# Expert rows by indirect DMA, five column-group products per row block, whole-row weights and halved mixer products in a hybrid decoder trunk

## The chip, the core and the metric

The kernel runs on one core of a Trainium2 chip. The metric is the device time of one launch in microseconds (us), as the median of several runs. Everything is computed in float32, and one launch does both layers.

## What is computed

There are two layers over 256 tokens of width 1024. Each layer has an RMSNorm, an input projection, four groups of token mixers, an output projection and a residual add, then a second norm and a feed-forward part: dense in the first layer, and in the second layer the best two of eight experts for every token. A final RMSNorm follows.

```python
def reference(x, ...):                       # x: (1, 256, 1024)
    for l in range(2):
        h = rmsnorm(x, attn_norm[l]); proj = h @ w_in[l]
        ...                                  # A window attention, B gated linear attention,
        ...                                  # C stick breaking, D RWKV-7, on 256 columns each
        x = x + mixed @ w_out[l]
        h = rmsnorm(x, ffn_norm[l])
        x = x + (swiglu(h, w1, w3, w2) if l == 0 else moe_swiglu(h, router, ...))
    return rmsnorm(x, final_norm)

def moe_swiglu(h, router, w1, w3, w2):
    top_vals, top_idx = lax.top_k(h @ router, 2)
    gates = jax.nn.softmax(top_vals)
    combine = ...                            # (tokens, 8): the gate, or zero
    for e in range(8):                       # w1, w3: 1024 x 1408, w2: 1408 x 1024
        out += combine[:, e:e+1] * ((silu(h @ w1[e]) * (h @ w3[e])) @ w2[e])
    return out
```

## The kernel before

Each engine runs a program of its own, written out by hand; the engines meet through semaphores. `full[b]` counts how often PSUM bank b has been filled, `free[b]` how often it has been emptied, and `nth(i, b, k)` is the count that belongs to the k-th use of bank b in round i of the expert loop. TensorE works through its list in order of the code; `mm` is the helper that records a product, so most products carry its line, L518. A float32 product shows as two weight loads and two matmul records in the profile.

**The mixers** (`layer_mixers`, `recurrence`, once a layer) are a long chain of small products. Many of them have 128 x 128 weights and only 64 columns of data: in `CO` (12 products), `GO` (8), `AO` (12), `RH0` and `RH1` (4 and 8), `U0` and `U1` (4 each), `Y0` and `Y1` (8 and 12), which is 72 products a layer; `BON` has 4 more with 2 columns. The router product `RT` (second layer alone) has 16 with 8 columns.

**The expert loop** (`experts` on TensorE, lines 975 to 1080) has one round per expert and pass; there are as many passes as are needed for 96 slots (`CAP`) per expert. In a round TensorE does four things:

- up: for each of the 11 blocks of 128 columns of w1 and w3, 8 + 8 products against `slot_h`, the 96 gathered tokens, each split in two halves of 64 output rows that stand at rows 0 and 64 of the bank (so 352 products in all);
- two transposes of `weigh` (the one-hot matrix with the gates, 256 tokens x 96 slots), and the gather for the next expert, 32 products of `tok` with the one-hot `pick`;
- down: for each of the 11 row blocks of w2, two products with 96 slots as output rows and 512 columns, into banks 2 and 3;
- the way back (`SCATTER`): four products of `weigh_t` with `slot_y`, 512 columns each, whose results VectorE adds to `x_sb`, the residual stream.

ScalarE takes the silu of one block at a time and VectorE multiplies it by the other factor. SyncE's queue loads the weights in pieces of 256 columns of w1 or w3 (lines of 1 KB) and of two row blocks of w2 (lines of 4 KB), through nine slots (`expert_slot`), each of which is loaded again when its last product is done.

Of the kernel before, what the change touches and what calls it, by code (L numbers as in the profile page):

```python
# [14 lines left out]
HALF = 64  # L15
D = 1024
# [37 lines left out]
MAX_PASSES = -(-SEQ // CAP)  # L54

# [3 lines left out]
for _name, _n in (("ident", 128), ("rev_cum", 128), ("rev_all", 128), ("c_mask", 128), ("a_mask", 256),  # L59
                  ("upper", 256), ("lower", 128), ("blk16", 128), ("off32", 128), ("off64", 128),  # L60
                  ("off128", 128), ("gla_mask", 64), ("same_head", 128), ("head_sel", 2),
                  ("reset64", 256), ("reset128", 512), ("inv_freq", 32), ("all", 128),
                  ("iota", CAP)):
    CONST[_name] = (_at, _n)
    _at += _n
# [19 lines left out]
def shape_constants():  # L85
# [25 lines left out]
    put("iota", np.arange(CAP)[None, :])  # L111
    put("inv_freq", (np.float32(ROPE_THETA) ** (-np.arange(0, HD, 2, dtype=np.float32) / np.float32(HD)))[None, :])
# [27 lines left out]
def psum_plan():  # L140
# [9 lines left out]
    for l in range(DEPTH):  # L150
# [24 lines left out]
        else:  # L175
            for name, bank in (("RT", 6), ("POS", 7), ("G0", 6), ("G1", 7)):
                use(name, l, bank)
# [16 lines left out]
def build(nc, t_in, out):  # L194
    ctx = ExitStack()
    with ctx:
# [13 lines left out]
        ring = sb("ring", [P, SLOTS, SLOT])  # L210
        region_e = sb("region_e", [P, 8192])
        region_f = sb("region_f", [P, 4096])
        region_g = sb("region_g", [P, 3072])
        region_m = sb("region_m", [P, 5128])
        normed = sb("normed", [P, 2, 512])
        ar = sb("ar", [P, 2, 2, NT, 256])
        c_q = sb("c_q", [P, 2, 2, SEQ])
        b_q = sb("b_q", [P, 4, SEQ])
        b_att = sb("b_att", [P, NT, 4, P])
        a_k = sb("a_k", [P, 2, SEQ])  # L220
# [85 lines left out]
        final_row = region_f[:, 1024:2048]  # L306

        W = MAX_PASSES * N_EXPERTS + N_EXPERTS
        slot_act = region_e[:, 0:UPC * CAP].rearrange("p (c s) -> p c s", c=UPC)
        slot_silu = region_f[:, 0:2 * CAP].rearrange("p (b s) -> p b s", b=2)  # L310
        slot_h = region_m[:, 0:KC * CAP].rearrange("p (c s) -> p c s", c=KC)
        pick = region_m[:, 768:768 + NT * CAP].rearrange("p (t s) -> p t s", t=NT)
        weigh = region_m[:, 960:960 + NT * CAP].rearrange("p (t s) -> p t s", t=NT)
        weigh_t = region_m[0:CAP, 1152:1152 + SEQ].rearrange("p (t n) -> p t n", t=NT)
        slot_y = region_m[0:CAP, 1408:1408 + D]
        place = region_m[:, 2432:2432 + NT * W].rearrange("p (t i) -> p t i", t=NT)
        chosen = region_m[:, 2432 + NT * W:2432 + 2 * NT * W].rearrange("p (t i) -> p t i", t=NT)
        share = region_m[:, 2432 + 2 * NT * W:2432 + 3 * NT * W].rearrange("p (t i) -> p t i", t=NT)
        count = region_m[:, 3072:3072 + N_EXPERTS]
        most = region_m[:, 3080:3088]  # L320
# [12 lines left out]
        descend = sb("descend", [P, N_EXPERTS])  # L333

# [47 lines left out]

        MORE = 3
        SLOTS_E = SLOTS + MORE
        more_slots = region_e[:, 8192 - MORE * SLOT:8192].rearrange("p (s n) -> p s n", s=MORE)
        more_landed = [ctx.enter_context(nc.semaphore(f"more_slot{i}_landed")) for i in range(MORE)]

        def expert_slot(k, n):

            r = k % SLOTS_E  # L390
            return ring[:, slot(FIRST_MOE + r), 0:n] if r < SLOTS else more_slots[:, r - SLOTS, 0:n]

        def expert_landed(i, k):

            r = k % SLOTS_E
            before = (FIRST_MOE + r) // SLOTS if r < SLOTS else 0
            s = landed[slot(FIRST_MOE + r)] if r < SLOTS else more_landed[r - SLOTS]
            return s, i * (16 * (E_PIECES // SLOTS_E)) + 16 * (before + k // SLOTS_E + 1)

# [4 lines left out]
        E_PIECES = 3 * UP2  # L404
        assert E_PIECES % SLOTS_E == 0


        per = [(UPC + 1) // 2, UPC // 2, 3, 2, 1, 1, 1, 1]
# [12 lines left out]
        def _(sp):  # L421
# [42 lines left out]
            def expert_piece(e, k):  # L464
                if k < 2 * UP2:
                    i = k // 2
                    m = min(256, D_FFE - 256 * i)
                    w = t_in["moe_w1" if k % 2 == 0 else "moe_w3"]
                    src = w[0, e].rearrange("(c p) n -> p c n", p=P)[:, :, 256 * i:256 * i + m]
                    dst = expert_slot(k, KC * m).rearrange("p (c n) -> p c n", n=m)  # L470
                else:
                    i = k - 2 * UP2
                    m = min(2, UPC - 2 * i)
                    src = t_in["moe_w2"][0, e].rearrange("(c p) n -> p c n", p=P)[:, 2 * i:2 * i + m, :]
                    dst = expert_slot(k, m * D).rearrange("p (c n) -> p c n", n=D)
                sp.dma_start(dst, src).then_inc(expert_landed(e, k)[0], 16)

            def expert_released(i, k):
                if k < 2 * UP2:
                    j = min(2 * (k // 2) + 1, UPC - 1)  # L480
# [1458 lines left out]
```

## Time and profile before

| | |
|---|---|
| median of 3 runs | 1143.0 us (1141.84 to 1143.22) |
| profiled execution | 1143.13 us, of which 1141.3 us from its first to its last instruction |
| TensorE busy | 1102.5 us of 1141.3 |
| granted TensorE clock, mean | 0.982 |
| start of the expert loop's first product | 689.28 us |
| one round of the expert loop | 55.09 us |
| time after the loop's last product | 9.63 us |

The time outside the profiled span is 1143.13 - 1141.3 = 1.8 us. Times in the rows of the profile count from the start of the span.

### The profile page before, as it was taken

The numbers are of one execution on the slowest core, as the hardware profiler recorded it, in microseconds if no ns is written. First come the engines' busy times: TensorE is split into PE (matmuls) and PEld (weight loads), VectorE is DVE, ScalarE is ACT, GpSimd is POOL, SyncE is SP. The second block draws the span as 40 slices with busy tenths as digits, with TensorE's granted clock in tenths as the row PEclk, the third lists the DMA queues.
The fourth block names the chain that finished last, engine by engine and source line by source line (L and its number), as shares of the span: only waits on it lengthen the run. The fifth ranks groups of instructions, "written<-read, shape, count | busy, mean of one in ns | idle before, by whom it ended". The sixth has DMA issues, their size and how long they took to land.

```text
span 1141.3 us, 22432 instructions
## 1 busy us (share of the span) xinstructions
PE 1102.5 (97%) x9790; PEld 837.2 (73%) x9790; DVE 285.3 (25%) x645; ACT 192.9 (17%) x444; POOL 61.4 (5%) x67
## 2 busy tenths in 40 slices
PE   8999999899999999999999969999999999999996
PEld 6887887488888543887789549595949494949592
DVE  4432473500000001233376341020111112021112
ACT  2244231100000001214323011011010111101011
POOL 2000411000000000000312100000000000000000
PEclk8999999999999999999999989999999999999998
DMA  9633101335554445343210256989898989899870
GB/s 325 196 122 105 43 1 38 111 117 160 160 159 167 156 148 155 119 135 109 74 38 1 74 185 203 343 279 351 287 344 289 343 293 323 305 301 332 279 272 37
DMA packets 168650, 213.34 MB, mean 187 GB/s; under 512 B 5120, under 2 KB 151200, under 8 KB 168480
## 3 DMA queue, kind: packets, MB, share of 16 engines
q1 hardware_dynamic: 166032, 210.29, 56.0%
q10 hardware_dynamic: 2576, 2.45, 0.7%
q8 instruction: 32, 0.52, 0.2%
q14 instruction: 10, 0.08, 0.0%
HBM read 211.67 MB, written 1.05 MB: 186 GB/s over the span
## 4 chain that ended last, share of the span: by engine, by line
PE 95%; DVE 3%; issue 1%; ACT 1%; POOL 0%; DMA 0%; DVEq 0%; POOLq 0%; ACTq 0%
PE bank L518 93%; PE bank L523 1%; DVE tok L1434 1%; POOL small L1343 0%; DMA x_sb<-in_x 0%; DVE b_att L1616 0%; DVE b_q L1413 0%; PE bank L1045 0%; DVE x_sb L1410 0%; PE bank L829 0%; ACT tok L1121 0%; DVE small L1425 0%; ACT hT L1133 0%; DVE hT L1410 0%; PE bank L797 0%
## 5 line engine op out<-in xcount | busy, mean ns | idle before, releaser
L518 PE MATMUL bank<-hT,ring 128*128 128x256 f32 (+1 forms) x1184 | 260.3, 382 | 0.0
L518 PEld LDWEIGHTS bank<-hT,ring 128*128 128x128 f32 (+1 forms) x1184 | 223.4, 189 | 36.1 <-issue 2.7
L518 PEld LDWEIGHTS bank<-region_m,ring 128*64 128x64 f32 x4096 | 170.3, 137 | 8.6 <-issue 8.6
L518 PE MATMUL bank<-region_m,ring 128*64 128x96 f32 x4096 | 173.7, 246 | 2.9 <-DVE region_m L1860 1.6
L518 PE MATMUL bank<-ring,region_e 128*96 128x512 f32 (+1 forms) x368 | 160.0, 594 | 0.0
L518 PEld LDWEIGHTS bank<-ring,region_e 128*96 128x96 f32 (+1 forms) x368 | 64.1, 176 | 89.5 <-issue 88.5
L518 PE MATMUL bank<-ring,hT 128*128 128x256 f32 (+1 forms) x448 | 127.8, 442 | 1.4 <-ACT hT L1138 1.4
L518 PE MATMUL bank<-region_e 128*128 128x128 f32 (+2 forms) x512 | 119.2, 384 | 0.0
L1410 DVE TENSOR_TENSOR region_e<-region_f,bank 128x96 f32<-128x96 f32 (+1 forms) x110 | 31.7, 288 | 341.7 <-ACT region_f L1318 198.9
L518 PEld LDWEIGHTS bank<-ring,hT 128*128 128x128 f32 x448 | 84.0, 190 | 35.7 <-issue 25.8
L518 PEld LDWEIGHTS bank<-region_e 128*128 128x128 f32 (+1 forms) x512 | 71.9, 191 | 46.9 <-issue 46.8
L518 PE MATMUL bank<-region_m,region_e 128*64 128x96 f32 x1536 | 66.1, 246 | 0.0
L518 PEld LDWEIGHTS bank<-region_m,region_e 128*64 128x64 f32 x1536 | 64.4, 137 | 0.0
L1318 ACT ACTIVATE region_f<-bank 128x96 f32<-128x96 f32 x88 | 22.1, 251 | 234.8 <-PE bank L518 234.8
L1343 POOL TENSOR_TENSOR small<-small 128x1 f32<-128x1 f32 (+1 forms) x18 | 18.6, 1034 | 800.5 <-DVE small L1425 738.8
L1410 DVE TENSOR_TENSOR x_sb<-x_sb,bank 128x512 f32<-128x512 f32 x44 | 30.3, 689 | 93.5 <-PE bank L518 93.5
L518 PE MATMUL bank<-region_f 128*128 128x128 f32 (+1 forms) x352 | 43.0, 275 | 0.0
L518 PEld LDWEIGHTS bank<-region_f 128*128 128x128 f32 x352 | 41.2, 192 | 1.6 <-issue 1.6
L1880 DVE COPY region_m<-bank 96x512 f32<-96x512 f32 x8 | 5.5, 686 | 144.4 <-PE bank L518 144.4
L1296 ACT ACTIVATE region_f<-bank 128x256 f32<-128x256 f32 x22 | 8.4, 384 | 138.6 <-PE bank L518 138.6
L518 PE MATMUL bank<-region_m 96*128 96x512 f32 x64 | 30.4, 617 | 0.0
L523 PE MATMUL bank<-consts,tok 128*128 128x128 f32 x96 | 17.0, 323 | 13.5 <-DVE tok L1434 13.5
(234 smaller groups left out, 715.0 us busy)
## 6 DMA issues: line engine op xcount, KB each, us to landing
ring<-in_moe_w SPq DMA_DIRECT2D x80, 1024.0 KB, 6.9
region_e<-in_moe_w SPq DMA_DIRECT2D x40, 1024.0 KB, 6.8
ring<-in_ffn_w SPq DMA_DIRECT2D x33, 1024.0 KB, 5.4
ring<-in_w_in SPq DMA_DIRECT2D x22, 1024.0 KB, 5.4
ring<-in_w_out SPq DMA_DIRECT2D x8, 1024.0 KB, 4.9
ring<-in_moe_w SPq DMA_DIRECT2D x16, 512.0 KB, 5.8
region_e<-in_moe_w SPq DMA_DIRECT2D x8, 512.0 KB, 4.0
ring<-in_w_in SPq DMA_DIRECT2D x2, 1088.0 KB, 5.5
```

Of the source, the lines that this page charges most:

```text
L518: return nc.tensor.matmul(o, lhsT, rhs, start=start, stop=stop, skip_group_check=True)
L523: last = nc.tensor.transpose(bank(name, l)[:, cc * 256 + t * P:cc * 256 + t * P + P], tok[:, t, (2 * c2 + cc) * P:(2 * c2 + cc + 1) * P], ...
L1296: nc.scalar.activation(silu_tmp[:, j % 2, :], bank(f"up{j}", l)[:, 0:SEQ], ACT.Silu).then_inc(sem("silu"), 1)
L1318: nc.scalar.activation(slot_silu[:, b, :], banks[b][:, 0:CAP], ACT.Silu).then_inc(sem("moe_silu"), 1)
L1343: g.tensor_tensor(ap_out, ap_in, m_half[:, 0:n], ALU.pow).then_inc(sem("rstd_ready"), 1)
L1410: return v.tensor_tensor(o, a, b, op)
L1434: v.tensor_scalar(tok[:, t, s], x_sb[:, t, s], scale, None, ALU.mult).then_inc(sem("h_ready"), 1)
L1880: v.tensor_copy(slot_y[:, 512:1024], banks[3][0:CAP, :]).then_inc(free[3], 1)
```

## The change

There are four parts.

**Expert rows by DMA.** Before the loop ScalarE's queue stores the normed tokens to `h_rows` and the residual stream to `x_rows`, both in HBM (the latter with 96 spare rows that empty slots write to). For each expert two small products (`place_rows`, 2 columns) turn the one-hot `pick` into a token number and a gate per slot; VectorE makes integers of the numbers (`next_rows`); GpSimd's queue fetches the 96 rows by an indirect DMA into `slot_rows`, and TensorE turns them into features with eight transposes (`rows_to_slots`) ahead of the last three row blocks of down. The 32 gather products of a round go. The result rows are multiplied by the gate while they are copied out of PSUM, and a second indirect DMA adds them to `x_rows`. The four products of the way back and the two transposes go from the loop; they stand once behind it, for the last expert, after `x_sb` has been loaded back from `x_rows`.

**Down in five products per row block.** 96 slots x 1024 columns are covered by slots 0-63 x columns 0-511 (output rows 0-63 of bank 5), slots 64-95 x columns 0-511 (rows 64-95), slots 64-95 x columns 512-1023 (rows 96-127), and slots 0-63 x columns 512-767 and 768-1023 (rows 0-63 and 64-127 of bank 6).

**Weights as whole row blocks.** w1 and w3 come as 128 whole rows of 1408 columns (lines of 5.6 KB), 8 + 8 pieces an expert, w2 in two row blocks as before. Each piece has its own place, so that one whole expert (17.3 MB) fits; the place is loaded for the next expert when its products are done. The up products run over row blocks outside and column blocks inside, with all 22 column blocks open in banks 0, 1, 4, 2 and 3, and silu and multiplication come once per bank, 480 columns wide.

**Mixer products in halves.** `CO`, `GO`, `AO`, `RH`, `U`, `Y`, `BON` and `RT` are recorded by `mm_halves`: two products with 64 output rows each in place of one with 128.

```diff
+            def mm_halves(o, lhsT, rhs, start=False, stop=False):
+                for q in range(0, P, HALF):
+                    last = mm(o[q:q + HALF, :], lhsT[:, q:q + HALF], rhs, start=start, stop=stop)
+                return last
...
-                    mm(o[:, c], a_pt[:, 4 + s, :], a_v[:, 0, v])
-                    last = mm(o[:, c], a_pt[:, 8 + s, :], a_v[:, 1, v], stop=True)
+                    mm_halves(o[:, c], a_pt[:, 4 + s, :], a_v[:, 0, v])
+                    last = mm_halves(o[:, c], a_pt[:, 8 + s, :], a_v[:, 1, v], stop=True)
...
+                def down_row(k):
+                    def product(o, s0, s1, c0, c1):
+                        return mm(o, slot_act[:, k, s0:s1], rows_b[:, k, c0:c1], start=(k == 0), stop=(k == UPC - 1))
+                    product(banks[5][0:HALF, :], 0, HALF, 0, 512)
+                    product(banks[5][HALF:CAP, :], HALF, CAP, 0, 512)
+                    product(banks[5][CAP:P, :], HALF, CAP, 512, D)
+                    low = product(banks[6][0:HALF, 0:GW], 0, HALF, 512, 768)
+                    high = product(banks[6][HALF:P, 0:GW], 0, HALF, 768, D)
+                    return low, high
+                def place_rows(o):
+                    for t in range(NT):
+                        last = mm(o, pick[:, t, :], pair[:, t, :], start=(t == 0), stop=(t == NT - 1))
+                    return last
+                def rows_to_slots(b, c0):
+                    for c in range(4):
+                        last = nc.tensor.transpose(banks[b][:, c * CAP:(c + 1) * CAP],
+                                                   slot_rows[:, (c0 + c) * P:(c0 + c + 1) * P], ident[0:CAP, 0:CAP])
+                    return last
...
+                    pe.wait_ge(sem("picks"), i + 2)
+                    place_rows(banks[7][0:CAP, 0:2]).then_inc(full[7], 1)
...
+                    for k2 in range(ROWS_B):
+                        pe.wait_ge(b_landed[k2], 16 * i + 16)
...
+                        if k2 == ROWS_B - TAIL:
+                            pe.wait_ge(free[7], nth(i, 7, 1))
+                            pe.wait_ge(sem("gathered"), 16 * i + 16)
+                            rows_to_slots(7, 0).then_inc(full[7], 1)
+                            pe.wait_ge(free[0], nth(i, 0, 1))
+                            rows_to_slots(0, 4).then_inc(full[0], 1)
...
+            def fetch_rows(i):
+                pool.wait_ge(free[7], nth(i, 7, 1))
+                g.indirect_dma_start(slot_rows, None, h_rows, bass.IndirectOffsetOnAxis(rows_in[:, 0:1], 0)).then_inc(
+                    sem("gathered"), 16)
+            with pool.Fori(0, n * N_EXPERTS - 1) as i:
+                fetch_rows(i)
+                pool.wait_ge(free[5], nth(i, 5, 1))
+                pool.wait_ge(free[6], nth(i, 6, 1))
+                g.indirect_dma_start(x_rows, bass.IndirectOffsetOnAxis(rows_out[:, 0:1], 0), slot_y, None,
+                                     compute_op=ALU.add).then_inc(sem("scattered"), 16)
+                pool.wait_ge(sem("scattered"), 16 * i + 16)
+                pool.sem_inc(sem("rows_added"), 1)
...
+                        dve.wait_ge(sem("rows_added"), i + 1)
                         dve.wait_ge(full[7], nth(i, 7, 1))
+                        v.tensor_copy(rows_out[:, :], rows_next[:, :])
+                        v.tensor_copy(gate_now[:, :], gate_next[:, :]).then_inc(sem("rows_moved"), 1)
+                        dve.wait_ge(sem("rows_moved"), i + 1)
+                        next_rows(banks[7][0:CAP, 0:2]).then_inc(free[7], 1)
...
+                for k in range(ROWS_A):
+                    if k < ROWS_A - 2:
+                        sp.wait_ge(sem("moe_row_used"), i * (KC - 1) + k // 2 + 1)
+                    else:
+                        sp.wait_ge(full[3], nth(i, 3, 1))
+                    expert_row_a((i + 1) % N_EXPERTS, k)
```

On TensorE, in a round behind the up products, stood the transposes of `weigh`, the gather, down and the way back (region_m holds `weigh`, `pick` and the slots, tok the tokens, ring and region_e the weights):

```order
L1045 MATMUL bank2<-consts,region_m 96x128 x2
L518 MATMUL bank6<-region_m,tok 64x96 x16
L518 MATMUL bank7<-region_m,tok 64x96 x16
L518 MATMUL bank2<-ring,region_e 96x512 x2
L518 MATMUL bank3<-ring,region_e 96x512 x2
...
L518 MATMUL bank4<-region_m 128x512
L518 MATMUL bank5<-region_m 128x512
```

Now there stand the two small products, eleven times the five products of a row block, and the eight transposes behind the eighth (arena is the one tensor that now holds weights and slots, and tok the fetched rows):

```order
L542 MATMUL bank5<-arena 64x512
L542 MATMUL bank5<-arena 32x512 x2
L542 MATMUL bank6<-arena 64x256 x2
L1130 REGISTER_ALU
L1070 MATMUL bank7<-consts,tok 128x96 x4
L1133 REGISTER_ALU
L1070 MATMUL bank0<-consts,tok 128x96 x4
```

So outputs of 64 and of 32 rows now alternate in every row block, and 36 products per round (gather and way back) are out of the loop.

On VectorE stood, from the last multiplication of a round to its end, the copy of the gathered slots, one copy of results, and the four additions to `x_sb`:

```order
L1410 TENSOR_TENSOR region_e<-region_f,bank0 128x96
L1875 REGISTER_ALU
L1860 TENSOR_SCALAR region_m<-bank7,params 128x96 x4
L1879 ISA
L1880 COPY region_m<-bank3 96x512
L1882 REGISTER_ALU
L1410 TENSOR_TENSOR x_sb<-x_sb,bank4 128x512
```

Now there stand the multiplication of bank 3, the five small steps that the fetch waits for, the slots, and three copies with a multiplication by the gate:

```order
L1520 TENSOR_TENSOR arena<-arena,bank3 128x480
L2006 REGISTER_ALU
L2007 COPY rows_out<-rows_next 96x1
L2008 COPY gate_now<-gate_next 96x1
L1981 TENSOR_SCALAR rows_next<-bank7,consts 96x1
L1982 TENSOR_SCALAR rows_in<-bank7 96x1
L1983 COPY gate_next<-bank7 96x1
L2011 REGISTER_ALU
L1972 TENSOR_SCALAR arena<-bank0,params 128x96 x4
L2015 REGISTER_ALU
L2016 REGISTER_ALU
L2017 COPY arena<-bank5 32x512
```

The additions to `x_sb` have gone from the round, and the row numbers of the next expert now pass through VectorE's queue.

## Rows read from the trace of the kernel before

**Rows 1.** The page: busy time by engine, and the chain that ended last.

```profile
PE 1102.5 (97%) x9790; PEld 837.2 (73%) x9790; DVE 285.3 (25%) x645; ACT 192.9 (17%) x444; POOL 61.4 (5%) x67
PE 95%; DVE 3%; issue 1%; ACT 1%; POOL 0%; DMA 0%; DVEq 0%; POOLq 0%; ACTq 0%
```

**Rows 2.** Busy time by stage: stretch, its us, engines, granted clock, DMA share, GB/s.

```profile
456.00:689.28 233.28, 218.67 (x1210) 176.03 (x1211) 101.56 (x224) 63.10 (x128) 26.48 (x22) 0.96 0.30 93
...
746.02:801.11 55.09, 55.09 (x824) 40.37 (x823) 8.29 (x24) 6.03 (x18) 0.00 (x0) 1.00 0.94 316
801.11:1131.67 330.56, 330.56 (x4933) 242.17 (x4932) 49.71 (x144) 34.91 (x107) 0.00 (x0) 1.00 0.86 288
1131.67:1141.30 9.63, 0.00 (x1) 0.00 (x0) 4.17 (x9) 2.56 (x8) 1.08 (x2) 0.64 0.29 109
```

**Rows 3.** Timeline of TensorE over the second expert: start, us, what.

```profile
746.02 16.06 PE L518 MATMUL bank<-region_m,ring 128*64 128x96 f32 x384
...
775.21 0.42 PE L1045 MATMUL bank<-consts,region_m 128*96 128x128 f32 x2
775.57 2.86 PE L518 MATMUL bank<-region_m,tok 128*64 128x96 f32 x64
778.36 10.54 PE L518 MATMUL bank<-ring,region_e 128*96 128x512 f32 x24
...
797.37 3.80 PE L518 MATMUL bank<-region_m 96*128 96x512 f32 x8
801.11 1.13 PE L518 MATMUL bank<-region_m,ring 128*64 128x96 f32 x22
```

**Rows 4.** Timeline at 481.9 us, products with 64 contraction rows, LW then LA.

```profile
481.90 0.48 PE L518 MATMUL bank<-region_m,lora 64*128 64x256 f32 x1
481.91 0.48 PE L518 MATMUL bank<-region_e,lora 64*128 64x256 f32 x1
...
482.22 0.38 PE L518 MATMUL bank<-region_m,lora 64*128 64x256 f32 x1
...
482.23 0.38 PE L518 MATMUL bank<-region_e,lora 64*128 64x256 f32 x1
...
482.44 0.38 PE L518 MATMUL bank<-region_m,lora 64*128 64x256 f32 x1
```

**Rows 5.** Timeline at 576.5 us, where the output rows change from 128 to 64 and back.

```profile
576.48 0.44 PE L708 MATMUL bank<-consts,hT 128*128 128x128 f32 x2
...
576.85 1.08 PE L518 MATMUL bank<-b_q,hT 128*64 128x256 f32 x8
...
577.87 0.38 PE L518 MATMUL bank<-region_e 128*128 128x128 f32 x1
```

**Rows 6.** Timeline of small products: transposes, AO and its successor, the router.

```profile
614.05 1.04 PE L829 MATMUL bank<-consts,region_m 128*128 128x128 f32 x8
...
618.93 2.79 PE L518 MATMUL bank<-region_m,hT 128*128 128x64 f32 x24
621.56 0.33 PE L518 MATMUL bank<-region_e 128*128 128x128 f32 x1
...
671.22 4.85 PE L518 MATMUL bank<-router_sb,hT 128*128 128x8 f32 x32 [1.05 <-ACT hT L1133]
```

**Rows 7.** DMA: two stretches (as rows 2), and page's issues: KB, us to landing.

```profile
820.00:830.00 10.00, 10.00 (x248) 10.00 (x246) 1.02 (x4) 0.86 (x4) 0.00 (x0) 1.00 1.03 410
900.00:910.00 10.00, 10.00 (x24) 3.69 (x23) 1.72 (x3) 1.86 (x2) 0.00 (x0) 1.00 1.05 333
...
ring<-in_moe_w SPq DMA_DIRECT2D x80, 1024.0 KB, 6.9
...
x_sb<-in_x SPq DMA_DIRECT2D x2, 512.0 KB, 4.4
```

**Rows 8.** Timeline of VectorE at the end of the second expert's down.

```profile
797.52 0.69 DVE L1880 COPY region_m<-bank 96x512 f32<-96x512 f32 x1 [18.05 <-PE bank L518]
798.53 0.69 DVE L1410 TENSOR_TENSOR x_sb<-x_sb,bank 128x512 f32<-128x512 f32 x1 [0.32 <-PE bank L518]
```

More of the change, by code:

```diff
@@ L15 @@
 HALF = 64
+QUARTER = 32
+TAIL = 2
 D = 1024
@@ L54 @@
 MAX_PASSES = -(-SEQ // CAP)
+EMPTY = 1024
+W = MAX_PASSES * N_EXPERTS + N_EXPERTS
+PARTS = {}
+ARENA = 0
+for _name, _n in (("ring", SLOTS * SLOT), ("e", 8192), ("f", 4096), ("g", 3072), ("m", 5128), ("normed", 1024),
+                  ("ar", 2048), ("c_q", 1024), ("b_q", 1024), ("b_att", 1024), ("a_k", 512)):
+    PARTS[_name] = (ARENA, _n)
+    ARENA += _n
+ROWS_A = 2 * KC
+ROWS_B = 6
+MOE_PARTS = {}
+_at = 0
+for _name, _n in (("rows_a", ROWS_A * D_FFE), ("rows_b", UPC * D), ("act", UPC * CAP), ("silu", UPC * CAP),
+                  ("h", KC * CAP), ("pick", NT * CAP), ("placed", NT * CAP), ("placed_t", SEQ), ("y", D),
+                  ("place", NT * W), ("chosen", NT * W), ("share", NT * W), ("pair", NT * 2), ("count", N_EXPERTS), ("most", 8),
+                  ("final", D)):
+    MOE_PARTS[_name] = (_at, _n)
+    _at += _n
+assert _at <= ARENA
 CONST = {}
@@ L1042, in experts @@
-                    pe.wait_ge(sem("weighs"), i + 1)
-                    pe.wait_ge(free[2], nth(i, 2, 0))
-                    for t in range(NT):
-                        last = nc.tensor.transpose(banks[2][0:CAP, t * P:(t + 1) * P], weigh[:, t, :], ident)
-                    last.then_inc(full[2], 1)
-                    pe.wait_ge(sem("picks"), i + 2)
-                    gather(i, (nth(i, 6, 0), nth(i, 7, 0)))
-                    pe.wait_ge(free[2], nth(i, 2, 1))
-                    pe.wait_ge(free[3], nth(i, 3, 0))
@@ new lines, in experts @@
+                    low.then_inc(full[5], 1)
+                    high.then_inc(full[6], 1)
+                n = n_passes * N_EXPERTS
+                for t in range(NT):
+                    last = nc.tensor.transpose(banks[1][0:CAP, t * P:(t + 1) * P], placed[:, t, :], ident)
+                last.then_inc(sem("placed_flipped"), 1)
+                pe.wait_ge(sem("placed_back"), 1)
+                pe.wait_ge(free[5], nth(n, 5, 0))
+                pe.wait_ge(free[6], nth(n, 6, 0))
+                for b, t, half in SCATTER:
+                    mm(banks[b][:, :], placed_t[:, t, :], slot_y[:, half * 512:(half + 1) * 512],
+                       start=True, stop=True).then_inc(sem("last_sums"), 1)
@@ L1885, in _ @@
-                        for b, t, half in SCATTER:
-                            dve.wait_ge(free[b], nth(i, b, per[b]))
-                    for t in range(2 * NT):
-                        v.sem_inc(sem("x_updated"), 1)
+                        one_hot(placed, i, chosen)
+                        one_hot(pick, i + 1, chosen)
+                        for t in range(NT):
+                            last = v.tensor_scalar(pair[:, t, 1:2], const("all")[:, 0:1],
+                                                   share[:, t, bass.ds(i + 1, 1)], None, ALU.mult)
```

387 lines of the change are left out of this document (212 added, 175 removed).

## The prediction, made before the run

> **What bounds the kernel now.** First the page's engine shares and its chain: TensorE is busy 97% of the span and holds 95% of the chain that ended last; no DMA is on it [rows 1]. Busy shares average over stages, so next the table by stage: a whole expert round, 55.09 us, has 55.09 us of matmul at a granted clock of 1.00, and the later six take 330.56, six times the same [rows 2]. The second layer's mixers and router are busy 218.67 of 233.28 us, at 93 GB/s. So in both parts that the change touches the order and price of matmuls sets the time, as long as weights arrive; the DMA engines are busy 0.94 of an expert round already, and a shorter round asks more of them.
>
> Then TensorE's own timeline over one expert [rows 3], as differences of starts: up 29.19 us (775.21 - 746.02), transposes of weigh 0.36, gather 2.79, down 19.01 (797.37 - 778.36), way back 3.74 to the next round: 55.09.
>
> **Gather and way back.** Out of a round go 0.36 + 2.79 + 3.74 = 6.89 us. In come: two products with 2 columns, four records at the 0.11 us that small records of 128 output rows take (eight transposes' records in 614.05 to 614.92; 24 of AO in 2.63) [rows 6], with their change of shape 0.6; eight transposes, 16 records at 0.11, with two changes of shape 2.05; 0.15 for the change into the next up. Sum 2.80, so all of a round but down costs 29.19 + 2.80 = 32.0 us. That change of shape: the products at 576.85 are eight records of 256 columns and 64 output rows in two alternating places; such records follow each other at 0.216 (482.22, 482.44 [rows 4]), four pairs side by side would be 0.86, and it takes 1.02 until the 128-row product at 577.87 [rows 5]: 0.16 us for a change of shape. I use 0.15.
>
> **Down.** Today 44 records of 512 columns in 19.01 us: 0.43 a record, 1.73 a row block. Does the engine run parts of the array side by side? Up says so: 352 products, 704 records of 96 columns, in 29.19, which is 0.083 for a pair of records. The sharper rows are LW and LA: in the program both LW products stand ahead of LA, yet LA's first record starts 0.01 after LW's first, and its second with LW's second [rows 4]. Each part of the array takes its own work, past up to three waiting records of the other part. So I count per part, for a row block: output rows 0-63 have 2 records of 512 and 2 of 256 columns, 2 x 0.43 + 2 x 0.216 = 1.29 us; rows 64-95 and 96-127 have the same each. Lower bound 1.29. But rows 64-127 change from two parts of 32 to one of 64 and back. If only that half pays, its chain is 1.29 + 2 x 0.15 = 1.59. The rows hold no change between two partial shapes: each one priced has the full array on one side. I take 1.36, nearer the lower end, because what the rows do show (LW and LA) is that a start depends on its own part alone, and the left half's chain of 1.29 pays nothing. Eleven blocks: 15.0 (14.2 to 17.5). Round: 47.0 us (46.2 to 49.5).
>
> The Trainium skill (TensorEngine Tiling (Array Packing), Tiling Modes, Key Properties) says that changing the tiling mode, not just the tile, drains the whole engine. By that rule a row block would be two phases that share nothing, the second rival below; the priced changes agree with a drain [rows 5], but none of them can tell a drain of all parts from a wait for the parts in use.
>
> **What hides the rest.** The fetch of the next rows starts when VectorE has multiplied bank 3 (0.69 for 512 columns [rows 8]) and done five small steps, some 2 us after up's end; its rows are wanted eight row blocks later, 0.75 + 8 x 1.36 = 11.6. It has 9.6 us, where 512 KB took 4.4 and 1 MB between weights 6.9 [rows 7]; these are 393 KB. On VectorE the wait for `rows_added` stands ahead of those steps, and behind it the fetch, the slots and thus the next up; the addition that it waits for is issued at the start of the round, 29 us before. GpSimd's two DMAs stand in one queue, but the addition goes out only after the fetch has been used. The copies of results (three and a multiplication, about 2.2 us at the 0.69 of [rows 8]) are hidden by up in all rounds but the last. Silu and multiplication per bank (0.7 each) are covered by the four blocks of up that follow and the small products; uncovered they would cost about 1 us a round. Weights: 17.3 MB and 1.2 MB for fetch and addition (read, read, write) are 18.5 MB a round; the stretch where w2's 4 KB lines land moves 410 GB/s [rows 7], so 45.1 us, under 47.0. The lines of w1 and w3 grow from 1 KB (333 GB/s) to 5.6 KB. Each place has nearly a round to be filled, so order and late releases cost nothing while the sum fits. The stores ahead of the loop, 2.4 MB, lie beside the first up.
>
> **Sum for the loop.** Now: 1131.67 - 689.28 = 442.4 us. After: 8 x 47.0 = 376.0, and behind it once 2.2 for the copies, 0.4 for transposes, 3.8 for the way back: 382.4. Gain 60.0.
>
> **Mixers.** 72 + 4 products a layer go to halves. A product takes 0.22 (24 records of AO in 2.63 us [rows 6]), although 64 columns stream in half the time that 128 do at the same 0.11: the load of 128 columns of weights sets it. As halves it is two pairs of records, 0.055 each if the pair's 0.083 shrinks with 64 for 96 columns, 0.083 if not: 0.11 to 0.17. I take 0.12, since half as wide a load is what each part then waits for. 76 x 0.10 = 7.6 a layer, less nine excursions into another shape (GO already stands beside one) at 0.3: 4.9, for two layers 9.8. The router's 32 records of 0.15 [rows 6] halve: 4.85 to 2.7, gain 2.1. Together 11.9; TensorE waits for others in 15 of 233 us there [rows 2], some of the gain will turn into such waits: 10 (0 to 14).
>
> **Total** against the profiled execution's 1143.1: -60 - 10 = 1073 us; that execution stands 0.1 over the median, so the forecast for the median is 1073.
>
> **The rivals.**
> - *The forecast*: parts side by side, weights in time. Own range 1063 (1.29 a block: 8 x 46.2 + 6.4 = 376.0; mixers 14) to 1093 (1.59 a block: 8 x 49.5 + 6.4 = 402.4). Chance 0.57.
> - *Every change between 64 and 32 empties the engine.* In a block: outputs of 64, both 256-column products side by side 0.43 and the next block's first 0.86; outputs of 32 side by side 0.86; two changes 0.30: 2.45 us. Eleven are 27.0, a round 59.0, the loop 478.4, 36 more than now; with the mixers' 10, 1169. It decides from 2.16 a block on, (442.4 + 10 - 6.4)/8 = 55.75, less 32.0, over 11. For it: no overlap across a change of shape is seen in any row. Against: LW and LA passing each other. Chance 0.20. This is the one on the other side.
> - *The fetch comes late.* Issue by GpSimd with row numbers from SBUF is in no row. At twice the 6.9 us of 1 MB it would be 4.2 late, each round: 34 us, 1107. It decides beyond 9.6. Chance 0.10.
> - *The weights bound.* If 5.6 KB lines, fetch and addition together move only the middle of 333 and 410, 371 GB/s, a round needs 49.9, seven times: 1093; at 333 it would be 55.5. It decides under 394 GB/s, which is close to 410, but the row with the longer lines speaks against it. Chance 0.10.
> - The mixers gain nothing or lose by their excursions: +10 on any of these; counted in their ranges. Others: 0.03.
>
> **Range and chances.** The drained engine stays outside (0.20). The other cases reach from 1058 to 1107, and with their bounds (half-late fetch on 1.59, mixers at 0) to 1118; at the low end, if the small products of a round take 2.0 in place of 2.8, to 1057. So 1057 to 1118. Faster by over 0.2% (2.3 us, about what a measurement of this kernel can tell) 0.79, within it 0.01, slower 0.20.
>
> **What the changed profile would show.** Eleven row blocks of down between the small products and up in 14 to 17.5 us: the forecast; 27: the rival. Starts of the 32-row products with the 64-row one of the same block, not after it. The transposes starting without an idle wait: the fetch is in time; idle time ended by a DMA before them: late. Up's 704 records in 29 us with no idle time ended by a DMA: weights in time; DMA share near 1 and idle in up: they bound. AO's 48 records in 1.4 us. The forecast is wrong if a block takes over 1.6 us or TensorE's idle time in a round is over 1 us.

## The result and the profile after

The changed kernel takes 1194.99 us (median of 4 runs, 1190.97 to 1202.18), the kernel before 1142.8 (1141.84 to 1143.22): ratio 1.0465, 95% interval 1.0414 to 1.0515. It is slower by 52 us, where 1073 was forecast. The profiled execution took 1194.63.

From the page of the changed kernel (busy time; DMA queues: packets, MB, share; chain; first group of instructions with its idle time):

```profile
span 1192.8 us, 22822 instructions
...
PE 1124.5 (94%) x10172; PEld 801.1 (67%) x10172; DVE 271.8 (23%) x638; ACT 180.0 (15%) x373; POOL 79.1 (7%) x82
...
q8 instruction: 98, 1.61, 0.5%
...
PE 92%; issue 3%; DVE 3%; ACT 1%; POOL 0%; DMA 0%; DVEq 0%; POOLq 0%; ACTq 0%
...
L542 PE MATMUL bank<-arena 128*64 128x96 f32 (+7 forms) x7932 | 668.3, 292 | 34.4 <-issue 31.4
```

Against [rows 1], "issue" has come up in the chain: TensorE stood still for 31.4 us with nothing in the profile to wait for. And the instruction queue has 98 packets, where the page of the kernel before has this:

```profile
q8 instruction: 32, 0.52, 0.2%
```

The table by stage of the changed kernel (columns as in [rows 2]; cut at the starts of rounds 1, 2, 3, 4 and 8, at the loop's end and the span's end):

```profile
677.81:740.29 62.48, 58.31 (x827) 37.00 (x827) 4.43 (x20) 3.71 (x8) 1.12 (x1) 1.00 0.96 378
740.29:805.28 64.99, 59.81 (x828) 38.73 (x828) 6.36 (x22) 4.39 (x9) 2.46 (x2) 0.97 0.80 281
805.28:868.96 63.68, 58.72 (x828) 37.00 (x827) 6.52 (x23) 4.59 (x10) 2.38 (x2) 1.00 0.82 286
868.96:1119.48 250.52, 235.90 (x3305) 151.34 (x3305) 25.13 (x88) 17.14 (x36) 9.48 (x8) 0.99 0.84 291
1119.48:1178.96 59.48, 57.83 (x830) 37.09 (x828) 6.33 (x22) 4.28 (x9) 2.37 (x2) 1.00 0.20 60
1178.96:1192.80 13.84, 3.97 (x10) 1.45 (x9) 8.15 (x16) 3.83 (x10) 1.11 (x2) 0.80 0.20 76
```

The loop starts at 677.81, 11.5 us earlier than before [rows 2]: the mixers did what was forecast. But a round takes 59.5 to 65 us in place of 55.09, 1.7 to 5.2 us of it without a matmul. In the rounds from the second on that load weights the DMA engines move 281 to 291 GB/s only, and the idle time is "issue", not a wait for a landing, so it is not the rate of the weights that binds. Two things are in a round. The first is down. Single rows of TensorE's timeline, one row block of w2 and the start of the next:

```profile
712.55 1.07 PE L542 MATMUL bank<-arena 128*64 128x512 f32 x2
713.55 1.05 PE L542 MATMUL bank<-arena 128*32 128x512 f32 x4
714.54 0.65 PE L542 MATMUL bank<-arena 128*64 128x256 f32 x4
715.02 1.02 PE L542 MATMUL bank<-arena 128*64 128x512 f32 x2
```

The starts tell it: the 32-row products stand 1.00 us behind the 64-row one, not beside it, and the next 64-row products 0.99 behind them. Only within one shape do the parts run side by side (4 records of 512 columns in 0.99, 4 of 256 in 0.48). From 715.02 on the row blocks follow each other every 2.417 us, eleven are 26.6 us, where 15.0 was forecast.

The second is up. The chain of the second round's up (start, us, what; it shows where TensorE stood still):

```profile
740.99 0.51 PE bank L542 x13
741.50 1.85 issue
743.35 17.71 PE bank L542 x383
761.06 0.28 issue
761.34 5.50 PE bank L542 x128
766.84 0.97 issue
767.81 5.50 PE bank L542 x128
773.31 2.07 issue
775.38 4.72 PE bank L542 x52
```

The stops lie 128 matmul records apart (383 is three times 128, less one). With the weight loads these are 256 instructions, which at the 64 bytes that follow from it are the 16 KB of one packet of queue q8. The packets' times in the trace say the rest: in the kernel before the queue brings six in the first round and then none; in the changed kernel it brings nine in this round, and nine from each jump of the loop to the next. The stops that end at 743.35, 767.81 and 775.38 end 1.2 to 1.5 us after one has landed (at 742.1, 766.5 and 773.9), and all 28 stops of over 0.2 us in the loop end 1.2 to 1.8 us after a landing. The loop no longer stays where TensorE reads its instructions.

### The profile page after: what moved, and what is told of

It is laid out like the page before. It is cut to its first block, busy times and chain, and to the rows that moved or that the text cites. A ratio compares the mean times of both kernels' runs of the same rounds, so it can differ in the third digit from the quotient of the medians.

```text
span 1192.8 us, 22822 instructions
## 1 busy us (share of the span) xinstructions
PE 1124.5 (94%) x10172; PEld 801.1 (67%) x10172; DVE 271.8 (23%) x638; ACT 180.0 (15%) x373; POOL 79.1 (7%) x82
## 4 chain that ended last, share of the span: by engine, by line
PE 92%; issue 3%; DVE 3%; ACT 1%; POOL 0%; DMA 0%; DVEq 0%; POOLq 0%; ACTq 0%
PE bank L542 90%; PE bank L553 1%; DVE tok L1544 1%; PE bank L1070 1%; POOL small L1430 0%; DMA x_sb<-in_x 0%; DVE arena L1520 0%; DVE arena L1726 0%; DVE arena L1523 0%; DVE x_sb L1520 0%; PE bank L859 0%; ACT hT L1210 0%; ACT tok L1198 0%; DVE small L1535 0%; PE bank L827 0%
## 5 line engine op out<-in xcount | busy, mean ns | idle before, releaser
L542 PE MATMUL bank<-arena 128*64 128x96 f32 (+7 forms) x7932 | 668.3, 292 | 34.4 <-issue 31.4
L542 PEld LDWEIGHTS bank<-arena 128*64 128x64 f32 (+3 forms) x7932 | 436.5, 144 | 263.1 <-issue 245.4
L542 PE MATMUL bank<-hT,arena 128*128 128x256 f32 (+1 forms) x1184 | 259.8, 382 | 0.4 <-ACT hT L1210 0.4
L542 PEld LDWEIGHTS bank<-hT,arena 128*128 128x128 f32 (+1 forms) x1184 | 223.5, 189 | 35.9 <-issue 3.1
L542 PE MATMUL bank<-arena,hT 128*128 128x256 f32 (+4 forms) x572 | 138.3, 406 | 5.7 <-DVE arena L1726 3.7
L1520 DVE TENSOR_TENSOR arena<-arena,bank 128x512 f32<-128x512 f32 (+3 forms) x90 | 51.1, 577 | 395.9 <-ACT arena L1403 238.1
L542 PEld LDWEIGHTS bank<-arena,hT 128*128 128x128 f32 (+2 forms) x572 | 90.1, 180 | 42.8 <-issue 26.3
L1215 ACT COPY arena<-bank 128x512 f32<-128x512 f32 (+2 forms) x66 | 37.4, 566 | 166.6 <-PE bank L542 160.3
L1520 DVE TENSOR_TENSOR arena<-arena 128x512 f32<-128x512 f32 (+3 forms) x50 | 31.3, 646 | 28.3 <-ACT arena L1215 27.5
L1520 DVE TENSOR_TENSOR x_sb<-x_sb,bank 128x512 f32<-128x512 f32 x16 | 11.0, 687 | 88.0 <-PE bank L542 87.9
```

What stands on the lines that cost most here:

```text
L542: return nc.tensor.matmul(o, lhsT, rhs, start=start, stop=stop, skip_group_check=True)
L1215: frees(nc.scalar.copy(dst, src), name, l)
L1520: return v.tensor_tensor(o, a, b, op)
```

## Experiments

Each ratio is to runs of the kernel before on the same chip, where its median was 1142.3 to 1144.4. A "fetch" is one packet of queue q8 in the whole launch.

### The place of the loop

A block is here 256 instructions, one packet. The expectations below count 1691 instructions of TensorE in the loop before and 1685 or 1686 in the changed one. They take a transpose as four instructions, like a float32 product. In the traces it is two (one weight load, one matmul record), so the loops have 1687 and 1670, as many as the traces hold from one jump to the next. Both are over six and a half blocks.

What differs is where they begin: the mixers in halves put some 680 instructions more ahead of the loop. In the changed kernel's trace the stops of up lie behind the loop's first 52 instructions and every 256 from there. So the loop begins at 256 - 52 = 204 of a block, ends at 204 + 1670 = 1874 and reaches 82 instructions into an eighth block (seven are 1792). For the loop before, the first stops of the runs `before_pad128` and `before_mix` below (behind 93 and 61 instructions) both give a begin at 35, so it ended at 1722, inside the seventh. Padding moves the loop without touching it. Two waits share one instruction:

```diff
                 fills(last, "RT", l)
+                for _ in range(200):           # 256 and 512 in the two with the kernel before
+                    pe.wait_ge(landed[0], 16)
```

> The changed kernel with 100 more instructions on TensorE ahead of the expert loop (waits that are long satisfied, placed where TensorE waits for VectorE's gates), and nothing else. In the changed kernel's trace the up products take 34 to 37 us where 29.2 were forecast; 27 idle gaps of 0.6 to 2.3 us stand 128 matmul records apart, and each ends as a 16 KB packet of the instruction queue lands; the queue fetches 98 packets where before it fetched 32. Theory (place of the loop): by a count of its instructions the loop body (1686, against 1691 before) starts some 200 instructions into a 256-instruction block and so touches eight blocks, where the loop before touched seven and was fetched once. With 100 more ahead it starts near 45 of the next block and touches seven: no fetches after the first round, up back to about 29.2, rounds of 57.4 in place of 62.6, seven rounds by 5.2 = 36 us less, 1159 us (1150 to 1170). Rival (weights or rows late, the fetches a coincidence): the gaps stay, 1195. Down stays at 2.42 us a row block by both.

1161.33 us (ratio to the kernel before 1.0163, interval 1.0132 to 1.0193), 35 fetches. From the second round on a round takes 57.16. The padding was not free: the loop starts 6.7 us later than in the changed kernel.

> The kernel before with 128 more instructions of the same kind on TensorE ahead of its loop. Theory (place of the loop): its body, which started near 40 of a block and touched seven, now starts near 168 and touches eight; fetches return in every round, about 5 us a round from the second on: 1143 + 35 = 1178 us (1155 to 1185). Rival (body length or the 5.6 KB lines of the changed kernel matter, not the place): 1143.

1177.91 us (1.0285; 1.0241 to 1.0330), 87 fetches in place of 32.

> The control: 256 more instructions ahead of the loop of the kernel before, twice the padding, but the loop again starts near 40 of a block. Theory (place of the loop): fetches in the first round alone, 1143 us within 2. Rival (the padding itself costs time, or a longer program does): more than the run with 128.

1164.79 us (1.0186; 1.0149 to 1.0223), 33 fetches. The fetches are as the place of the loop has them. The time isn't 1143, because TensorE works off 256 padding instructions more slowly than I had thought: the loop's first product starts at 710.70, 21.4 us later than in [rows 2]. Less these, 1143.4. So twice the padding takes 13 us less than the single one, and the same loop is fast or slow by where it starts.

The changed kernel with the padding where TensorE waits for the first data:

```diff
             (after the WARM_UP products)
+            for _ in range(150):
+                pe.wait_ge(sem("zeros"), 1)
```

> The changed kernel with 75 instructions of padding at the program's start, where TensorE waits for the first data, in place of 100 ahead of the loop. The body should start near 25 of a block: seven blocks, about 35 fetches, rounds of 57.16 as with the 100, but without the 6.7 us by which those delayed the loop: 1161.3 - 6.7 = 1154.6 us (1151 to 1158). What is left above 1144 is then the price of down's five products (26.6 against 18.95 us a round).

1154.47 us (1.0101; 1.0069 to 1.0134). Its page and its table by stage (starts of rounds 1, 2 and 3, the loop's end, the span's end):

```profile
q8 instruction: 35, 0.57, 0.2%
...
L542 PE MATMUL bank<-arena 128*64 128x96 f32 (+7 forms) x7932 | 656.1, 289 | 5.3 <-issue 2.3
```

```profile
679.47:738.87 59.40, 57.94 (x826) 37.22 (x828) 4.43 (x20) 3.60 (x8) 1.12 (x1) 1.00 1.00 396
738.87:796.04 57.17, 57.17 (x829) 36.88 (x827) 6.33 (x22) 4.29 (x9) 2.54 (x2) 1.00 0.86 317
796.04:1139.03 342.99, 342.99 (x4958) 221.12 (x4954) 38.00 (x132) 25.73 (x54) 14.26 (x12) 1.00 0.75 274
1139.03:1153.10 14.07, 4.22 (x12) 1.61 (x10) 8.16 (x16) 3.84 (x10) 1.12 (x2) 0.82 0.20 75
```

75 instructions that do nothing take 40.5 us off the changed kernel, and no round from the second on has any idle time left. The "issue" idle falls from 31.4 to 2.3, and the same products are busy for 656.1 us in place of 668.3.

### The mixers alone

The kernel before with `mm_halves` in the mixers and the router, without and with that padding.

> The kernel before with one part of the change alone: the mixer and router products in halves (the expert loop is untouched). Theory (place of the loop): the halves themselves bring the 11.5 us by which the changed kernel's loop started earlier (677.8 against 689.3), but they add 672 instructions ahead of the loop, which then starts near 208 of a block and touches eight: the same fetches in every round as in the run with 128 instructions of padding, which cost 1177.9 - 1144.4 less some 10 us for the padding itself, so 23 us. 1144 - 11.5 + 23 = 1156 us (1150 to 1163), about 87 fetches. Rival (mixer halves cost nothing elsewhere): 1133.

1180.46 us (1.0317; 1.0300 to 1.0335), 98 fetches.

> The same with 75 instructions of padding on TensorE at the very start of the program, where it waits for the first data, so that the loop starts near 27 of a block and touches seven. Theory (place of the loop): 1144 - 11.5 = 1133 us (1130 to 1136), about 35 fetches. Rival (the halves slow something else): as the run without padding.

1131.24 us (0.9895; 0.9876 to 0.9914), 35 fetches. The halves bring 13.0 us (9.8 to 14.2), and where they stand alone they cost 49 by what they move the loop to. The size of that was missed by 24 us. The trace shows why. At the jump back to the loop's head TensorE stands still (timeline), and after it the granted clock is at its lower level (table by stage: PEclk, DMA share and GB/s are the last three):

```profile
793.33 3.80 PE L518 MATMUL bank<-region_m 96*128 96x512 f32 x8
800.77 1.55 PE L518 MATMUL bank<-region_m,ring 128*64 128x96 f32 x16 [3.64 <-issue]
```

```profile
795.00:800.70 5.70, 2.13 (x5) 0.59 (x4) 3.29 (x8) 0.00 (x0) 0.00 (x0) 0.90 0.91 296
800.77:803.00 2.23, 2.23 (x28) 2.21 (x28) 0.00 (x0) 0.00 (x0) 0.00 (x0) 0.50 0.06 18
803.00:806.00 3.00, 3.00 (x38) 2.75 (x36) 0.00 (x0) 0.00 (x0) 0.00 (x0) 0.50 0.03 5
806.00:810.00 4.00, 4.00 (x96) 4.00 (x94) 0.51 (x2) 0.50 (x2) 0.00 (x0) 0.95 0.02 4
```

0.50 is 1.2 GHz. A stop of 3.6 to 4.5 us is followed by some 5 us at half the clock, in every round: 6 to 7 us, where the whole excess is 49.2 over seven rounds. The DMA engines were busy around the stop (0.91) and all but idle only behind it (0.06), so how much of this stop is a queue behind weights stays open.

### Is it a queue behind the weights?

```diff
-                    expert_row_a((i + 1) % N_EXPERTS, k)
+                    expert_row_a((i + 1) % N_EXPERTS, k, P)
...
-                sp.dma_start(rows_a[:, k, :], w[0, e, (k // 2) * P:(k // 2 + 1) * P, :])...
+                sp.dma_start(rows_a[:, k, 0:n], w[0, e, (k // 2) * P:(k // 2 + 1) * P, 0:n])...
```

> The changed kernel, whose loop still stands across eight blocks, but in the loop the loads of w1 and w3 bring only the first 128 of each row's 1408 columns (the other columns keep the first expert's weights, so this leaves out the loading of most of w1 and w3 for seven experts): 10.5 of 17.3 MB a round go. Question: what makes TensorE wait in up, the instruction packets queueing behind the weights on the DMA engines, or the fetch itself? Theory Q (queueing): about 98 fetches, but the gaps go or shrink under 0.3 us, rounds near 57.5, 1195 - 36 = 1159 us. Rival F (a fetch takes its time whatever else moves, and a block of 256 instructions is used up in 128 x 0.041 = 5.3 us of up): gaps as in the changed kernel, over 1185. Between these: a part is queueing.

1173.17 us (1.0272; 1.0235 to 1.0309), between the two. Its page:

```profile
q8 instruction: 98, 1.61, 0.6%
...
L542 PE MATMUL bank<-arena 128*64 128x96 f32 (+7 forms) x7932 | 660.7, 289 | 19.2 <-issue 15.9
```

All 98 fetches are still there, with half of the idle time. What is left is mostly the stop behind the loop's first 52 instructions, 1.4 to 1.9 us in every round from the second on; most of the later ones are gone. Of the 40.5 us about 22 hang on the weights' traffic and 19 on the fetches themselves.

### Down

Two products of 96 rows per row block, in the changed kernel:

```diff
-                    product(banks[5][0:HALF, :], 0, HALF, 0, 512)
...
+                    low = product(banks[5][0:CAP, :], 0, CAP, 0, 512)
+                    high = product(banks[6][0:CAP, :], 0, CAP, 512, D)
```

> The changed kernel with down in two products per row block, 96 output rows and 512 columns each, as before the change (into banks 5 and 6; copies by ScalarE and VectorE, one each). Theory (every change between 64 and 32 output rows empties the engine): a row block falls from 2.42 to 1.73 us, eleven from 26.6 to 19.0, 8 x 7.6 = 61 us. The body is also 132 instructions shorter, so it touches seven blocks from where it stands: by the place of the loop another 36, 1195 - 61 - 36 = 1098 us (1088 to 1110), fetches in the first round alone. If the gaps in up are not of the fetches, they stay: 1134. If down's price is not of the changes of shape but of banks 5 and 6 being written at once, a row block stays over 2.2 us.

1089.05 us (0.9523; 0.9498 to 0.9548), 34 fetches. A round is 49.25 (table by stage, rounds 2 and 3 to 8), 7.9 under 57.16 where the row blocks alone were expected to give 7.6. The small products and the transposes take 1.16 in place of 1.43, probably because most of them now stand between products of their own shape:

```profile
729.82:779.07 49.25, 49.25 (x761) 37.14 (x760) 4.97 (x19) 4.28 (x9) 2.44 (x2) 1.00 1.02 400
779.07:1074.57 295.50, 295.50 (x4562) 223.08 (x4562) 29.81 (x114) 25.72 (x54) 14.27 (x12) 1.00 0.86 321
```

Is it the change of shape that keeps 64-row and 32-row products apart, or that three of the five write bank 5? The 32-row products moved to bank 1:

```diff
-                    product(banks[5][HALF:CAP, :], HALF, CAP, 0, 512)
-                    product(banks[5][CAP:P, :], HALF, CAP, 512, D)
+                    product(banks[1][HALF:CAP, :], HALF, CAP, 0, 512)
+                    product(banks[1][CAP:P, :], HALF, CAP, 512, D)
```

> The changed kernel with 75 instructions of padding at the start (1154.5 us without more), and the two products with 32 output rows of each row block moved from bank 5 to bank 1 (rows 64-127 there), so that no bank is written in both shapes. The next up may touch bank 1 only after the copies of the results, which adds 1 to 2.5 us a round. Theory (the change between 64 and 32 output rows holds up all parts of the array): a row block stays at 2.42 us, the whole is 1163 to 1175. Rival (the products with 64 and with 32 output rows stand one after the other because they write one bank): the 512-column product of rows 0-63 and those of rows 64-127 run side by side, a row block of 1.3 to 1.6 us, 8 x 11 x 0.9 = 80 less, about 1090.

1169.17 us (1.0234; 1.0203 to 1.0264), and the row block hasn't moved (timeline, as above):

```profile
770.15 1.02 PE L542 MATMUL bank<-arena 128*64 128x512 f32 x2
771.10 1.05 PE L542 MATMUL bank<-arena 128*32 128x512 f32 x4
772.09 0.65 PE L542 MATMUL bank<-arena 128*64 128x256 f32 x4
772.57 1.02 PE L542 MATMUL bank<-arena 128*64 128x512 f32 x2
```

2.42 us again (772.57 - 770.15): it is the shape, not the bank.

If parts work side by side only in one shape, each shape has to fill the array by itself. Six products do: slots 0-63 as two of 64 rows, slots 64-95 as four of 32 rows. Both versions with 75 instructions at the start:

```diff
+                    if low:
+                        product(banks[5][0:HALF, :], 0, HALF, 0, 512)
+                        low = product(banks[5][HALF:P, :], 0, HALF, 512, D)
+                    if high:
+                        for q in range(4):
+                            high = product(banks[6][q * QUARTER:(q + 1) * QUARTER, 0:GW], HALF, CAP, q * GW, (q + 1) * GW)
...
+                        for wide in (True, False) if k2 % 2 == 0 else (False, True):   # grouped
+                            for k in pair_rows:
+                                done = down_row(k, low=wide, high=not wide)
```

> The same six products, not grouped: two changes of shape in every row block, 21 in a round in place of 6. Theory (a price per change): 1.29 + 0.21 = 1.50 us a row block, eleven 16.5, round 46.8, 1089 - 8 x 2.45 = 1070 us, 14 above the grouped order (if the weights don't bind that one). Rival (the price of a change is much larger than 0.1, or depends on what stands around it): more than 30 above the grouped order.

1081.19 us (0.9449; 0.9433 to 0.9465). One row block (timeline):

```profile
714.82 1.08 PE L542 MATMUL bank<-arena 128*64 128x512 f32 x4
715.83 0.64 PE L542 MATMUL bank<-arena 128*32 128x256 f32 x8
```

The next starts at 716.40, so a block is 1.58: 1.29 and 0.29 for two changes, 0.144 each. That is 0.08 a block over the expected 1.50, which makes 7 of the 11 us over the forecast 1070.

> The changed kernel with down in six products per row block: two with 64 output rows and 512 columns side by side (slots 0-63), four with 32 output rows and 256 columns side by side (slots 64-95), and grouped: both row blocks of a piece in the one shape and then both in the other, the next piece in reverse order, so six changes of shape for eleven row blocks. 75 instructions of padding at the program's start keep the body (1730) in seven blocks. Theory (a change of shape empties the engine and costs 0.09 to 0.12 us; within a shape the parts run side by side): a row block is 0.86 + 0.43 = 1.29, eleven are 14.2 + 6 x 0.1 = 14.8, against 18.95 in two products of 96 rows; a round 45.1 in place of 49.25: 1089 - 8 x 4.15 = 1056 us. At 45 us a round the 18.5 MB would need 410 GB/s, what the DMA engines reach at most in any stretch: if the weights bind now, a round is 46 to 48 and the whole 1063 to 1080, with waits for landings in up. Rival (four parts of 32 rows do not run side by side): 0.86 + 4 x 0.43 a block, over 1130.

1064.19 us (0.9303; 0.9288 to 0.9319), the fastest kernel here, 80 us under the one before. By stage (rounds 1, 2, 3 to 8, and what is left):

```profile
676.89:724.24 47.35, 46.23 (x849) 35.82 (x851) 4.42 (x20) 3.60 (x8) 1.12 (x1) 1.00 1.02 404
724.24:769.88 45.64, 45.64 (x851) 35.54 (x849) 7.94 (x25) 4.28 (x9) 2.44 (x2) 1.00 1.02 399
769.88:1043.72 273.84, 273.84 (x5090) 213.10 (x5086) 47.48 (x150) 25.69 (x54) 14.23 (x12) 1.00 0.93 361
1043.72:1062.30 18.58, 7.09 (x12) 2.69 (x10) 9.73 (x19) 3.83 (x10) 1.12 (x2) 0.67 0.15 56
```

The round is 45.64, 0.5 over the expected: half of that because each of the six changes costs 0.144 and not 0.1, the rest in the small products, which take 1.45 here and 1.16 with 96 rows (45.64 - 29.14 - 15.05 and 49.25 - 29.14 - 18.95, where 29.14 is up and 15.05 and 18.95 are the eleven row blocks). All of the round is matmul: the weights arrive in time even at 45.64, with the DMA engines full (1.02). The miss of 8 us is some 3 in the rounds and 5.6 in the end behind the loop, 18.58 against 12.93 in the version with 96 rows. I had left that end out. The last result is copied in more pieces, so TensorE waits 3.54 us for it in place of 0.99. Behind this wait its granted clock is 0.50 (from 1048 to 1050), and the way back takes 6.57 us in place of 3.69. Grouping is worth 17.0 us, 14 expected.

### Where is the edge?

The version with 96 rows (1538 instructions in the loop, with a transpose as two) and the changed kernel, with other amounts of padding at the start. Without padding both loops begin at 204 of a block.

> The version with down in two products of 96 rows (1554 instructions in the body, started near 206 of a block) with 20 instructions of padding at the program's start: it ends near 226 + 1554 = 1780 of seven blocks' 1792. Theory (place of the loop): as without padding, 1089 us (1087 to 1092), about 34 fetches.

1089.77 us, 34 fetches, as expected.

> The same with 45 instructions of padding in place of 20: 251 + 1554 = 1805, over the edge of 1792 into an eighth block. Theory (place of the loop): fetches in every round, 90 to 100 in all, and 25 to 45 us more than with 20: 1114 to 1134 us. Rival (the length of the loop in instructions decides, not the blocks that it touches): 1089.

1091.43 us, 34 fetches: the expectation missed. By the count of the traces the loop did not touch the eighth block: 204 + 45 + 1538 = 1787, five short of 1792.

> Down in two products of 96 rows, with 55 instructions of padding at the start. The run with 45 did not go over the edge: 34 fetches, 1091 us. Counted anew: in the changed kernel's later rounds the gap stands behind 24 weight loads and 24 matmul records, and the loop's head has 15 register and semaphore instructions, so the body starts 63 instructions ahead of a block's end, at 193 and not 206. With 45 it then ends at 193 + 45 + 1554 = 1792, just inside seven blocks; with 55 at 1802, ten instructions into the eighth. Theory (place of the loop): fetches in every round, 90 to 100, and 20 to 45 us more than with 45: 1111 to 1136. Rival (another limit, such as the body's length): 1091 again.

1089.79 us, 35 fetches. The recount behind this expectation was wrong too: 55 more put the loop's start just over a block's edge (204 + 55 - 256 = 3), and it ends at 1541.

> Where is the edge at which fetches return in every round? The changed kernel with 170 instructions of padding at the start. Its loop (1685 instructions) starts near 202 of a block without padding, so now near 116, and reaches some 10 instructions into an eighth block. Touching the eighth decides: about 98 fetches and 1180 to 1200 us. Reaching deep enough into the eighth for the ninth to be fetched decides (the changed kernel reaches 95 into it and fetches 98 times, the kernel before with 128 more reaches some 60 and fetches 87 times; two products of 96 rows with 45 more reached 9 and fetched 34 times): about 35 fetches and 1154 to 1157 us, as with 75.

1164.63 us, 35 fetches, rounds of 57.16. The time is over the expected, in part because so much padding isn't covered at the start (the loop starts 5.4 us later than with 75). The expectation has the loop some ten instructions into the eighth block. By the count of the traces it ends four instructions before it: 204 + 170 - 256 = 118, and 118 + 1670 = 1788. So this run does not show that a loop may reach into an eighth block.

> The same with 200: the loop reaches some 40 instructions into the eighth block. If touching decides: 98 fetches, 1180 to 1200 us. If depth decides, the edge lies between 10 and 60, and this run tells on which side of 40: 35 fetches and 1155 us, or over 80 fetches and 1175 to 1200 us.

1197.91 us (1.0503; 1.0471 to 1.0535). Its page:

```profile
q8 instruction: 99, 1.62, 0.6%
```

30 instructions more, and the fetches are back in every round: the loop begins at 148, ends at 1818 and reaches 26 instructions into the eighth block. In all runs the blocks that the loop touches decide: with seven or fewer 32 to 35 fetches, with eight 87 to 99. The edge lies between 4 instructions short of the eighth block and 26 into it, and no run narrows it further. The changed loop fetches nine packets a round, one more than it touches; whether it is this one that throws the first block out was only argued.

## Why the prediction was wrong

In the changed kernel's span against the 1141.3 before: loop 9.8 earlier (as measured with 75 at the start), eight rounds of 57.16 for 55.09, +16.6, the first round's own stops +0.6, the end behind the loop 14.07 for 9.63, +4.4. That gives 1153.1, the span of the run with 75. The fetches add 40 more. Against the forecast the measured time is 122 us over: 93 of them are down's row blocks and 40 the fetches, and the small products give 11 back.

- **Down, the step that failed first.** "I take 1.36, nearer the lower end, because what the rows do show (LW and LA) is that a start depends on its own part alone." It measured 2.417 a block: the parts are independent only while they have one shape. LW and LA have one shape, so those rows could not carry the step. This is 11 x 1.06 = 11.6 us a round, 93 in all. The rival with the drained engine, given 0.20, had 2.45 a block and 27.0 for eleven; measured 2.417 and 26.6. The rule in the Trainium skill (TensorEngine Tiling (Array Packing), Tiling Modes, Key Properties), that changing the mode drains the engine, holds in this trace, for parts that the next products don't use too. The price of a change, 0.15 from [rows 5], was right: 0.13 here and 0.144 in the ungrouped six.
- **Up, the step that isn't in the prediction at all.** 29.19 a round was taken over, "without idle time" named as the sign. Resident, it is 29.14 (28.96 to the last record's start, 0.18 to the next). In the changed kernel it was 31 to 37. The term missing is what 680 more instructions ahead of a loop do to the loop: 40.5 us. It can't be seen in [rows 1 to 8]; the page's line on q8 had the 32 packets, and their times would have shown that six came in the first round and none later.
- **Small products** 2.80 forecast, 1.43 measured (57.16 - 29.14 - 26.59). The eight transposes came as 8 records, 0.81 us in all, not as 16 of 0.11, and the two small products took 0.43 with their changes. [rows 3] already had two transposes as two records (L1045). The same slip went into the counts of instructions above.
- **Mixers** -10 forecast, -13.0 measured in the kernel before with the loop kept in place. Right, inside the stated 0 to 14.
- **Fetch and addition by DMA, weights as row blocks.** Right: no transposes that waited, no idle time in a round of 45.64 us, 399 to 404 GB/s in the first two rounds. The rivals of a late fetch and of bound weights are out.

Without the five products the rest of the change is good: 1089 against 1144. Part of that is luck, as this loop is 132 instructions shorter and so touches seven blocks from the same place.

## What to carry to other kernels

Ask of every shape by itself whether it fills the array: products of 64 and of 32 output rows don't share it, and a change costs about 0.14 us, so group by shape. Count the instructions of a long loop on TensorE, a float32 product as four and a transpose as two, and find where it starts: a loop that reaches 26 instructions or more into an eighth block of 256 was fetched again in every round here. An edit far ahead of the loop can move it there, and before such an edit is judged, the instruction queue's packets in the two profiles should be compared; a few idle instructions where the engine waits anyway put it back.

## What the hardware showed that I had not expected

- TensorE's instructions come in packets of 16 KB during the run. A loop of 1687 or 1670 instructions is fetched once when it lies within seven packets, and in every round when it touches eight (32 to 35 against 87 to 99 packets in a launch); the same kernel took 1154.5 or 1195.0 us by 75 instructions that do nothing.
- A stop of 3.6 to 4.5 us at the loop's jump is followed by some 5 us at a granted clock of 0.50, which costs more than half as much again.
- A wait that is long satisfied isn't free on TensorE: 256 padding instructions delayed the loop by 21.4 us, 0.084 us each on average.
